# Layers 1 and 4 of a decoder trunk: project the gate before v, and evacuate v later

## What is computed

```
proj = h @ w_in                      # 2048 x 8192
q, k, v, g = split(proj, 4 x 2048)
s = rope(q) rope(k)^T, causal        # 8 heads, two score maps each
pd = softmax(s_1) - lambda * softmax(s_2)
o = rmsnorm(pd @ v) * (1 - lambda_init)
y = (o * silu(g)) @ w_out
```

## Time and profile before

| | us |
|---|---|
| median of 3 runs | 1711.88 (1711.56 to 1712.52) |
| the profiled execution, its own time | 1712.57 |
| span of the profiled execution | 1710.8 |
| PE busy | 1699.6 (99%) |
| DVE busy | 1188.9 (69%) |
| ACT busy | 911.4 (53%) |

### The profile page before, as it was taken

One profiled execution on the slowest core, in us unless ns is written; L12 is line 12 of the kernel. 1 busy time (PEld: TensorE's weight loads), 2 busy tenths in 40 slices (PEclk: granted clock), 3 DMA queues, 4 the chain that ended last, 5 costly groups with the idle time before them and its releaser, 6 DMA issues.

```text
span 1710.8 us, 24445 instructions
## 1 busy us (share of the span) xinstructions
PE 1699.6 (99%) x7890; PEld 1417.7 (83%) x7890; DVE 1188.9 (69%) x1909; ACT 911.4 (53%) x1400; POOL 38.9 (2%) x99
## 2 busy tenths in 40 slices
PE   9999999999999999999999999999999999999998
PEld 7888888888888888888888888888888888888887
DVE  7767677775769888865656465656676676777756
ACT  7454555554656666655544545454554555455543
POOL 1000000000000000000000000000000000000000
PEclk9999999999999999999999999999999999999999
DMA  8768676766875555478998699966877686767673
GB/s 286 244 194 262 201 245 215 233 216 220 264 216 161 160 159 153 154 234 194 190 166 271 177 201 182 265 182 216 260 227 237 195 265 200 247 214 232 223 237 126
DMA packets 230035, 364.53 MB, mean 213 GB/s; under 512 B 14950, under 2 KB 80044, under 8 KB 229836
## 3 DMA queue, kind: packets, MB, share of 16 engines
q1 hardware_dynamic: 229536, 362.94, 73.5%
q0 software_dynamic: 48, 0.13, 0.1%
q10 hardware_dynamic: 380, 0.56, 0.1%
HBM read 335.79 MB, written 27.79 MB: 213 GB/s over the span
## 4 chain that ended last, share of the span: by engine, by line
PE 95%; DMA 2%; issue 1%; SPq 1%; DVE 1%; ACT 0%; DVEq 0%; POOLq 0%; POOL 0%; ACTq 0%
PE acc L1136 29%; PE acc L1137 29%; PE acc L1138 29%; PE tp L1102 1%; PE tp L1137 1%; PE tp L1136 1%; PE tp L1138 1%; DMA raw<-in_ml_w_in_dram 1%; PE sc L1137 1%; PE sc L1136 1%; PE sc L1138 1%; DMA xres<-in_x_dram 0%; DMA qs<-q_turning 0%; DMA q_turning<-scr 0%; PE sc L1162 0%
## 5 line engine op out<-in xcount | busy, mean ns | idle before, releaser
L2015 DVE TENSOR_TENSOR w_lo<-raw,w_hi 128x1024 fp32r<-128x1024 f32 x583 | 703.2, 1220 | 401.4 <-ACT w_hi L1074 399.0
L1074 ACT ACTIVATE w_hi<-raw 128x1024 fp32r<-128x1024 f32 x583 | 610.2, 1056 | 454.9 <-PE acc L1138 401.6
L1136 PE MATMUL acc<-w_hi,xt_hi 128*128 128x512 f32 x1824 | 715.3, 392 | 1.7 <-DVE w_lo L2015 1.0
L1138 PE MATMUL acc<-w_hi,xt_lo 128*128 128x512 f32 x1824 | 711.0, 390 | 0.0
L1137 PE MATMUL acc<-w_lo,xt_hi 128*128 128x512 f32 x1824 | 710.4, 389 | 0.0
L1138 PEld LDWEIGHTS acc<-w_hi,xt_lo 128*128 128x128 f32 x1824 | 342.4, 188 | 72.3
L1136 PEld LDWEIGHTS acc<-w_hi,xt_hi 128*128 128x128 f32 x1824 | 342.6, 188 | 70.3 <-DVE w_lo L2015 1.6
L1137 PEld LDWEIGHTS acc<-w_lo,xt_hi 128*128 128x128 f32 x1824 | 342.6, 188 | 67.3
L1136 PE MATMUL acc<-w_hi,ot_hi 128*128 128x512 f32 (+1 forms) x456 | 176.6, 387 | 0.0
L1138 PE MATMUL acc<-w_hi,ot_lo 128*128 128x512 f32 (+1 forms) x456 | 175.8, 386 | 0.0
L1137 PE MATMUL acc<-w_lo,ot_hi 128*128 128x512 f32 (+1 forms) x456 | 175.8, 385 | 0.0
(11 more groups left out here) (306 smaller groups left out, 1226.5 us busy)
## 6 DMA issues: line engine op xcount, KB each, us to landing
raw<-in_da_w_in_dram SPq DMA_DIRECT2D x255, 512.0 KB, 4.4
raw<-in_ml_w_in_dram SPq DMA_DIRECT2D x96, 512.0 KB, 5.7
raw<-in_sw_w_in_dram SPq DMA_DIRECT2D x72, 512.0 KB, 3.7
raw<-in_da_w_out_dram SPq DMA_DIRECT2D x64, 512.0 KB, 4.0
raw<-in_sw_w_out_dram SPq DMA_DIRECT2D x32, 512.0 KB, 3.7
raw<-in_ml_w_in_dram SPq DMA_DIRECT2D x64, 256.0 KB, 7.3
raw<-in_ml_w_out_dram SPq DMA_DIRECT2D x32, 512.0 KB, 3.9
qs<-q_turning SPq DMA_DIRECT2D x12, 512.0 KB, 6.9
```

The costliest lines, as they stand in the source:

```text
L1074: act.activation(w_hi[:, q:q + 2, :], raw[:, 2 * p:2 * p + 2, :], ACT.Copy).then_inc(hi_ready, 1)
L1136: pe.matmul(out_ap, k_hi, m_hi, start=start, stop=False)
L1138: return pe.matmul(out_ap, k_lo, m_hi, start=False, stop=stop)
L2015: dve.tensor_tensor(w_lo[:, two, :], raw[:, two, :], w_hi[:, q:q + 2, :].bitcast(F32), ALU.subtract).then_inc(lo_ready, 1)
```

## The change

Within an iteration of layers 1 and 4 the columns of the third and fourth job are exchanged: the gate is job 2 (slots 16 to 23), v is job 3 (slots 24 to 31). `g_tanh` moves from slot 35 to 27, `gate` from 36 to 28, and both parts of v's evacuation from 27 to 35. `pv` waits for job 3's banks in place of job 2's. Number and shape of all instructions and transfers stay.

```diff
-          v_evac=27, ...
-          g_tanh=35, gate=36, ...
+          v_evac=35, ...
+          g_tanh=27, gate=28, ...
...
-                                load(w_in, D * j + JW * i, J + j, also=also[j])
+                                load(w_in, D * (0, 1, 3, 2)[j] + JW * i, J + j, also=also[j])
...
-                    v_evac(l, job(i, 2), i, par, da_v_hi)
+                    v_evac(l, job(i, 3), i, 1 - par, da_v_hi)
...
-                    tanh_half(l, job(i, 3), i, 1 - par, th)
+                    tanh_half(l, job(i, 2), i, par, th)
...
-                        wait_emptied(pe, l, LOOP0[l] + 2, i)
+                        wait_emptied(pe, l, LOOP0[l] + 3, i)
...
-                    v_rest(l, i, par, da_v_hi, da_v_lo)
+                    v_rest(l, i, 1 - par, da_v_hi, da_v_lo)
...
-                    gate(l, LOOP0[l] + 4 * i + 3, i, 1 - par)
+                    gate(l, LOOP0[l] + 4 * i + 2, i, par)
```

More of the change, by code:

```diff
@@ L67 @@
 DA = dict(q_evac=11, q_turn=12, q_write=19, q_read=21, q_copy=20, k_evac=19, k_turn=20, k_write=27, k_read=29, k_copy=28,
-          v_evac=27, score=25, softmax=29, diff=(31, 33), p_turn=34, p_write=39, p_read=41, p_copy=40, pv=(37, 38), ssq=(41, 42),
-          g_tanh=35, gate=36, mix=45, o_write=50, o_read=52, o_split=54, o_split_last=51)
+          v_evac=35, score=25, softmax=29, diff=(31, 33), p_turn=34, p_write=39, p_read=41, p_copy=40, pv=(37, 38), ssq=(41, 42),
+          g_tanh=27, gate=28, mix=45, o_write=50, o_read=52, o_split=54, o_split_last=51)
 SW = dict(kv_evac=3, sink_set=10, v_stage=14, k_T=5, k_hi=9, k_lo=(10, 13), q_evac=11, q_T=11, q_hi=(15, 16), q_lo=(15, 15, 17, 18),
```

## The result

The changed kernel takes 1717.88 us (median of 6 runs, 1717.32 to 1718.58), the kernel before 1711.93 (6 runs). The ratio is 1.0034 with a 95% interval of 1.0024 to 1.0044, so the change costs 4.1 to 7.5 us, 5.8 in the middle. The profiled execution took 1717.73 with a span of 1716.0, 5.2 more than that of before. PE is busy 99% of the span as before, at the same clock, and its instructions are the same 7890 matmuls. What is new is that it waits. The first view is PE's waits in the changed kernel, in the window of layer 1 (60 to 440 us), and then of layer 4 (1260 to 1700): us in total, times, longest.

A forecast was written before the change was run, and what follows sets the result against it. PE was taken to set the time, with no wait to lose in layers 1 and 4; 1.26 + 1.41 + 1.80 = 4.47 us on the profiled 1712.57 gave 1717.04, or 1716.4 as median, range 1711.8 to 1719.6.

The forecast's parts named there:

- The sign and the place: Layers 1 and 4: slower by over 0.2% (70%), with PE waiting on `w_lo` at slots 32 and 33 of all eight iterations.
- No credit for `v_rest`: Slot 27 on DVE: removing two `v_rest` (1.41 us) gains nothing, since `w_lo` there waits for ACT's `w_hi`.
- The size: Layers 1 and 4, eight iterations: 1.26 + 1.41 + 1.80 = 4.47 us slower in all.
- the loop's lateness, 1.62: Slots 29 to 33: the maxima-exponentials loop starts 1.62 us late, the gate's 2.12 less the covered wait for the scores.
- The cost of a restart, 0.15: Each late slot on PE costs its lateness plus 0.15 us, from 0.38 between data and second matmul in layer 3.
- The variant without this cost: PE hides the weight load behind a wait, so 8 x 0.15 = 1.20 us less, 3.3 in all; given a seventh of the forecast's 70%.
- The spare lead at slot 35, 0.99: Slot 35, with `v_rest` now ahead of its `w_lo`: 0.99 us of lead left, so no PE wait.
- The spare lead at `pv`, 0.9: At `pv`: lead 2.05 us plus PE's delay 0.47, less at most 1.62, leaves 0.9; no wait, but next to be late.
- The rival that hung on it: Turned probabilities come 2.5 us or more late and PE stalls at `pv` too: about 1720, 8%.
- waits in other slots: The prediction's test: wrong if PE shows no waits on L2015 in layer 1, or waits outside slots 32 and 33.
- Hidden after all: Removing `v_rest` at slot 27 pays 1.41 of the gate's 2.12, the loop starts 0.28 late: no change, 1711.9 us, 15%.
- Less overlap on DVE: The gate's four instructions find no overlap at slot 28, loop up to 0.32 us later still: 2.6 more, 1719.0, 5%.

The follow-up runs named there:

- Experiment 1: The changed kernel with the gate on VectorE at slot 29 in place of 28: 1712.2 us against 1712.7 for the kernel before, ratio 0.9999.
- 3: The kernel before with two added DVE instructions (1.33 us together) at slot 28 behind `kT_hi`: 1713.24 us, ratio 1.0005.
- experiment 4: The kernel before with three added DVE instructions (2.00 us together by plan) at slot 28: 1716.53 us, ratio 1.0023.
- The trace without late landings: Profile of the changed kernel with `k_read` at slot 28 in place of 29; that kernel took 1717.10 us, ratio 1.0029 to the kernel before.
- the first changed trace: Profiled execution of the changed kernel itself in the main measurement: 1717.73 us; two landings of k were later than 2.4 us behind PE's slot 24.
- experiment 2: The changed kernel with the gate on VectorE at slot 27 in place of 28: 1716.99 us, ratio 1.0024 to the kernel before.
- The control: The kernel before with `k_read` at slot 28 in place of 29: 1712.15 us, ratio 0.9998.

## Why the prediction was right

**The sign and the place.** Right. PE had no wait to lose in these layers, and none of the eight kernels was faster than before beyond its interval. The loss lies at slots 32 and 33 of all eight iterations, by the mechanism described: 2.12 us ahead of a loop of two engines that has no spare wait, and a lead that ends at slot 33. Experiment 1 removes it by one slot, 3 and 4 make most of it in the kernel before by added work, with the threshold where the leads put it.

**No credit for `v_rest`.** Right, by the 2.73 us of idle time in its place, and by experiment 4.

**The size.** Forecast 4.47, measured 5.8 with 4.1 to 7.5 around it. The trace without late landings gives 5.2, so 0.7 was missing in the terms, while the 6.2 of the first changed trace has late landings of k in it. That such landings also make the difference in the medians was not shown (the intervals overlap). The mis-sized term is first the loop's lateness, 1.62: it was 1.60 in the two first iterations and 1.67 in the others. In these tanh starts 0.08 later behind PE than v's copies did (ACT idle 1.74 before it, 1.66 in the earlier trace rows). That fits the one more wait that the code has there in all iterations but the first; no run took it away. It makes 0.3 of the 0.7. Another 0.25 is lost behind the second matmul of slot 33, where the forecast counted nothing: in the trace with `k_read` at 28 the eight iterations together are 4.9 late at that matmul and 5.2 at the start of slot 34. The last 0.15, 0.02 in each iteration, is not resolved.

**The cost of a restart, 0.15.** Right to 0.01 as far as the second matmul: at slot 33 it began at 289.83, 0.39 behind the end of `w_lo`, where I had 0.38 from layer 3. Some 0.03 come behind it, as just said. The variant without this cost, 3.3 us in all, is out, by this 0.39 and by the 5.2 counted.

**The spare lead at slot 35, 0.99.** Measured 1.10 to 1.16. No wait.

**The spare lead at `pv`, 0.9.** Wrong, though without effect: it is 2.06 in the changed kernel, as it was, but for the last iteration (1.71). I let `p_lo` move with `p_turn`. It is held by the `w_hi` and `w_lo` of slot 39, which go at PE's pace, and `p_read` landed in time or nearly. The rival that hung on it had less for it than I gave it.

**What the prediction left out.** The scores' wait for `kT_lo`, with 0.63 of lead, and the transfer in front of it. The list of leads was made for `w_lo`, `p_lo` and `v_lo` and not for `kT_lo`. The prediction called itself wrong if PE "waits in other slots", and in this one place it did: PE lost 0.51 behind slot 25 in layer 4's second iteration. The control shows the same wait without the change (0.54 for a landing at 3.40, here 0.51 for one at 3.37), so it is no part of what the gate's move does. It cost little here, but it made the expectation of experiment 2 wrong by 4 us.

**Rivals.** Hidden after all: out, the maxima started 1.6 late or more. Less overlap on DVE: out, the gate took 2.12. `pv`: out.

## What to carry to other kernels

Where one engine is never idle, a move on the others is free up to the smallest lead behind it, and nothing is free beyond: list each wait of the busy engine with its lead, those for small operands too, and look which is the first behind the new place. Where an instruction waits for another engine, taking away the work that stood ahead of it gains nothing (`v_rest`), and work put there is covered only in part (the gate at 27 made `kT_lo` 0.9 late); work belongs into a wait that it fits, here behind the first maxima and not ahead of them, one slot apart and worth all of the 5.8 us. Using up a lead also takes the cover from transfers that sometimes land late, so in such iterations the loss is larger than the plain sum.

## What the runs showed of the hardware

A 512 KB read of turned data that took 6.6 us from issue to landing in the median of before took between 5.0 and 9.3 in the two profiled executions of the changed kernel, and in one place (layer 4's second iteration) it landed 2.6 us or more behind PE's slot 24 in half of the ten traces, whatever the kernel; why that one, no run shows. Issued one 512 KB weight load earlier, it had a median of 6.0 in the changed kernel, against 6.8 and 7.0 in the two executions without that.
